# Attention scores of two heads as one pair: 64-row tiles, two banks, maximum and shift for two units

## The reference, cut

```python
# sliding window attention (SWA), 8 query heads on 2 key heads of 64, window 128
s = einsum('bnqhgd,bnkhd->bnhgqk', qb, kk) * ATTN_SCALE
s = where(valid, s, NEG)
m = maximum(max(s, -1), sink)
p = exp(s - m);  p = p / (sum(p) + exp(sink - m))
# forgetting attention (fox), 8 heads of 64, causal
s = einsum('bqhd,bkhd->bhqk', q_blk, k) * ATTN_SCALE
s = s + c_blk[..., None] - c[:, :, None, :]
s = where(k_pos <= q_pos, s, NEG)
p = softmax(s);  o = einsum('bhqk,bkhd->bqhd', p, v)
```

## Time and profile before

| | us |
|---|---|
| median of 3 runs (1494.97 to 1495.83) | 1495.04 |
| span of the profiled execution | 1495.9 |
| TensorE busy | 1349.3 |
| VectorE busy | 479.2 |
| ScalarE busy | 264.3 |
| attention loop, first score load to first output transpose | 87.7 |

### The profile page before, as it was taken

How to read it: one execution, slowest core, us unless ns; L and a number is a source line. 1 busy time by engine, 2 the same in 40 slices (tenths; PEclk the granted TensorE clock), 3 DMA queues, 4 the chain that set the end, 5 groups by cost and what they waited for, 6 DMA issues and landing times.

```text
span 1495.9 us, 27925 instructions
## 1 busy us (share of the span) xinstructions
PE 1349.3 (90%) x11152; PEld 653.5 (44%) x11152; DVE 479.2 (32%) x1212; ACT 264.3 (18%) x452; POOL 168.6 (11%) x250
## 2 busy tenths in 40 slices
PE   6999998999969999989898898989889898989986
PEld 5998887878943333223232222323222232322221
DVE  4122747766354232222322222232222223222211
ACT  4223436433221011001011000101100011110001
POOL 2001401000010111111110111111011111101111
PEclk9999999999979999999999999999999999999998
DMA  6222320002658999999999999999999999999997
GB/s 183 85 84 85 107 90 1 1 29 85 254 208 309 390 407 401 402 402 406 404 401 411 395 408 402 407 403 403 409 397 407 402 406 404 404 408 397 407 401 244
DMA packets 112807, 458.14 MB, mean 306 GB/s; under 512 B 12129, under 2 KB 37761, under 8 KB 79969
## 3 DMA queue, kind: packets, MB, share of 16 engines
q1 hardware_dynamic: 102736, 433.87, 73.1%
q0 software_dynamic: 9344, 21.37, 5.9%
q10 hardware_dynamic: 688, 2.38, 0.4%
HBM read 442.90 MB, written 14.68 MB: 306 GB/s over the span
## 4 chain that ended last, share of the span: by engine, by line
PE 42%; DMA 27%; SPq 26%; DVE 2%; issue 2%; ACT 1%; POOL 0%; DVEq 0%; POOLq 0%; ACTq 0%
DMA gu_tail<-in_w_gate_up_dram 26%; SPq L474 15%; SPq L470 10%; PE ps L1607 8%; PE ps L1646 3%; PE ps L1342 3%; PE ps L1343 3%; PE ps L1344 3%; PE ps L1351 3%; PE ps L1352 3%; PE ps L1353 3%; PE ps L1438 2%; PE ps L1465 2%; PE ps L1652 1%; PE ps L1634 1%
## 5 line engine op out<-in xcount | busy, mean ns | idle before, releaser
L1607 PE MATMUL ps<-gu_head,xT 128*32 128x512 f32 x3840 | 440.0, 600 | 74.5 <-DMA gu_head<-in_w_gate_up_dram 70.0
L1607 PEld LDWEIGHTS ps<-gu_head,xT 128*32 128x32 f32 x3840 | 115.7, 110 | 392.2 <-issue 235.6
L1646 PE MATMUL ps<-wdn,aT 128*32 128x512 f32 x2048 | 237.9, 594 | 12.7 <-DMA wdn<-in_w_down_dram 10.8
L1166 DVE TENSOR_REDUCE row_f<-ps 128x2 f32<-128x4 f32 (+1 forms) x33 | 5.3, 161 | 525.8 <-PE ps L1572 525.8
L1607 PE MATMUL ps<-gu_tail,xT 128*32 128x512 f32 x1280 | 146.8, 595 | 16.4 <-DMA gu_tail<-in_w_gate_up_dram 16.3
L807 ACT COPY gu_tok<-ps 128x512 f32<-128x512 f32 x80 | 46.8, 585 | 621.3 <-PE ps L1607 621.3
L1646 PEld LDWEIGHTS ps<-wdn,aT 128*32 128x32 f32 x2048 | 62.0, 110 | 156.8 <-issue 126.3
L611 POOL DMA_INDIRECT xg_a<-h_dram,idx_g x33 | 33.3, 1008 | 580.2 <-DVE idx_all L1169 296.5
L860 DVE TENSOR_TENSOR st_l<-st_w,st_h 128x2048 fp32r<-128x2048 f32 x25 | 57.3, 2292 | 120.5 <-ACT st_h L683 120.5
L1607 PEld LDWEIGHTS ps<-gu_tail,xT 128*32 128x32 f32 x1280 | 37.1, 109 | 125.1 <-issue 63.5
L1342 PE MATMUL ps<-st_h,hT_h 128*128 128x256 f32 x288 | 82.4, 286 | 2.0 <-DVE hT_l L875 2.0
(11 more groups left out here) (337 smaller groups left out, 1588.9 us busy)
## 6 DMA issues: line engine op xcount, KB each, us to landing
gu_head<-in_w_gate_up_dram SPq DMA_DIRECT2D x192, 1024.0 KB, 21.1
wdn<-in_w_down_dram SPq DMA_DIRECT2D x128, 1024.0 KB, 26.7
gu_tail<-in_w_gate_up_dram SPq DMA_DIRECT2D x64, 1024.0 KB, 26.8
st_w<-in_w_in_dram SPq DMA_DIRECT2D x17, 1024.0 KB, 5.3
st_w<-in_w_out_dram SPq DMA_DIRECT2D x4, 1024.0 KB, 5.1
x_tok<-in_x_dram SPq DMA_DIRECT2D x4, 512.0 KB, 6.1
st_w<-in_w_o_swa_dram SPq DMA_DIRECT2D x4, 512.0 KB, 3.6
st_w<-in_w_o_fox_dram SPq DMA_DIRECT2D x4, 512.0 KB, 4.6
```

The source lines that it names most:

```text
L1607: ins = pe.matmul(ps[j * GROUP:(j + 1) * GROUP, n, :], xT[:, k, n * GROUP:(n + 1) * GROUP], gu_chunk(k)[:, j * 512:(j + 1) * 512], start=( ...
L1646: ins = pe.matmul(ps[u * GROUP:(u + 1) * GROUP, 4, :], aT[:, 2 * j + k, u // 2 * GROUP:(u // 2 + 1) * GROUP], wdn[:, j, k, u % 2 * 512:(u ...
```

## The change

The two heads of a pair (2p, 2p+1) are computed together. The wide query tiles go; `qaT` and `qfT` hold two heads one above the other, as the keys do, and each head's matmuls read and load only its 64 rows. The two heads write two banks, and their instructions alternate; from 384 columns on the scores come in pieces of 256 columns, below in pieces of 128. The bias comes first for fox, the mask first for SWA. `c_pick` gets its ones on the lower 64 rows also, by two more selects. One semaphore increment stands for both scores; VectorE takes the maximum over two banks and one shift for two units (`sink_neg` replaces `sink8`). `p_sb` has four buffers and lies elsewhere. The orders of TensorE and VectorE in the loop are new. A turned query block goes out as one block of 128 rows, and the zero fills are gone.

```diff
         def turned(s, j):
             bank = ps[:, QKT_BANK[QKT.index((s, j)) % 4], :]
-            if s % 2:
-                return [((None, kaT, None, kfT)[s][:, j, :], bank, 1.0 if s < 2 else g_fx[:, 1:2])]
-            out = []
-            for a in (0, 1):
-                rows = slice(a * HD, (a + 1) * HD)
-                out.append((wide_q(s == 2, 2 * j + a)[rows, :], bank[rows, :], 1.0 if s < 2 else g_fx[rows, 0:1]))
-            return out
+            return (qaT, kaT, qfT, kfT)[s][:, j, :], bank, (1.0, 1.0, g_fx[:, 0:1], g_fx[:, 1:2])[s]
...
-            for row in range(0, HD, 32):
+            for row in range(0, P, 32):
                 then(g.affine_select(out=c_pick[:, :], in_=c_pick[:, :], compare_op=ALU.not_equal, fill=1.0,
...
-            pool.wait_ge(group_done, G_O)
-            for half in (0, 1):
-                other = slice((1 - half) * HD, (2 - half) * HD)
-                for part in (qa_lo, qa_hi):
-                    g.memset(part[other, half::2, :], 0.0).then_inc(q_zeroed, 1)
...
             for n in range(NU):
-                act.wait_ge(shift, n + 1)
-                if n >= 3:
-                    act.wait_ge(pT_ps, n - 2)
+                act.wait_ge(shift, n // 2 + 1)
+                if n >= 4:
+                    act.wait_ge(pT_ps, n - 3)
...
-            for n in range(NU + 5):
-                if n < NU:
...
+            for p in range(NP + 3):
+                if p < NP:
+                    n = 2 * p
                     c, b, h = units[n]
-                    dve.wait_ge(scores, n + 1)
-                    v.reduce_max(mx[:, n:n + 1], ps[:, n % 4, 0:width(n)], AX.X).then_inc(maxed, 1)
...
+                    two, bank, w = slice(n, n + 2), n % 4, width(n)
+                    dve.wait_ge(scores, p + 1)
+                    v.tensor_reduce(mx[:, two], ps[:, bank:bank + 2, 0:w], AX.X, ALU.max).then_inc(maxed, 1)
+                    dve.wait_ge(maxed, p + 1)
                     if b == 0:
...
+                        v.scalar_tensor_tensor(out=nb[:, two], in0=mx[:, two], scalar=-SCALE, in1=sink_neg[:, h:h + 2],
+                                               op0=ALU.mult, op1=ALU.min).then_inc(shift, 1)
                     else:
...
+                        v.tensor_scalar(nb[:, two], mx[:, two], -SCALE, None, ALU.mult).then_inc(shift, 1)
...
+                if 1 <= p <= NP:
+                    for m in (2 * p - 2, 2 * p - 1):
+                        dve.wait_ge(pT_ps, m + 1)
+                        if m >= 2:
+                            dve.wait_ge(pv_done, m - 1)
+                        v.tensor_copy(pT_sb[:, m % 2, 0:width(m)], ps[:, 4 + m % 2, 0:width(m)]).then_inc(pT_ready, 1)
...
-            def unit_scores(n):
+            def pair_scores(p):
+                n = 2 * p
                 c, fox, h = units[n]
+                w = width(n)
                 k0 = (c + 1) * P - w
+                piece = 256 if w > 256 else P
+                if p >= 2:
+                    pe.wait_ge(probs, n - 2)
+                for a in (0, 1):
+                    rows, bank = slice(a * HD, (a + 1) * HD), (n + a) % 4
+                    if fox:
+                        pe.matmul(ps[:, bank, 0:w], c_pick_r[rows, h + a:h + a + 1].broadcast_to([HD, P]),
+                                  c_rows[rows, 0:w], start=True, stop=False)
+                    else:
+                        m = mask_b[:, :, :].rearrange("p a k -> p (a k)")[:, 2 * P - w:2 * P]
+                        pe.matmul(ps[:, bank, 0:w], ident_b[:, :], m, start=True, stop=False)
+                for at in range(0, w, piece):
+                    end = min(at + piece, w)
+                    for a in (0, 1):
+                        rows = slice(a * HD, (a + 1) * HD)
+                        q = (qfT if fox else qaT)[rows, h // 2, c * P:(c + 1) * P]
+                        kv = kfT[rows, h // 2, k0 + at:k0 + end] if fox else kaT[rows, h // (HQ // KV), k0 + at:k0 + end]
+                        ins = pe.matmul(ps[:, (n + a) % 4, at:end], q, kv, start=False, stop=(not fox and end == w))
                 if fox:
+                    for a in (0, 1):
+                        ins = pe.matmul(ps[:, (n + a) % 4, w - P:w], ident_b[:, :], mask_b[:, 1, :], start=False, stop=True)
                 ins.then_inc(scores, 1)
...
-            for n in range(NU + 3):
...
+            for p in range(NP + 2):
+                if p < NP:
+                    pair_scores(p)
+                if 1 <= p <= NP:
+                    unit_transposes(2 * p - 2)
+                if p >= 2:
+                    unit_values(2 * p - 3)
+                if 1 <= p <= NP:
+                    unit_transposes(2 * p - 1)
+                    unit_values(2 * p - 2)
```

More of the change, by code:

```diff
@@ L127, in hybrid_block @@
         stage.rewind(16 * K)
-        qa_lo = stage.put("qa_lo", [P, HQ // 2, T])
-        stage.rewind(32 * K)
-        qa_hi = stage.put("qa_hi", [P, HQ // 2, T])
+        qaT = stage.put("qaT", [P, HQ // 2, T])
         stage.rewind()
@@ L155, in hybrid_block @@
         kaT = r1.put("kaT", [P, KV, T])
-        qf_wide = r1.put("qf_wide", [P, HF, T])
+        qfT = r1.put("qfT", [P, HF // 2, T])
         kfT = r1.put("kfT", [P, HF // 2, T])
+        p_sb = r1.put("p_sb", [P, 4, T])
         r1.rewind()
@@ L190, in hybrid_block @@
         work.rewind()
-        p_sb = work.put("p_sb", [P, 3, T])
         pT_sb = work.put("pT_sb", [P, 2, T])
@@ L248, in hybrid_block @@
         sink_bc = const.put("sink_bc", [P, HQ])
-        sink8 = const.put("sink8", [P, HQ])
+        sink_neg = const.put("sink_neg", [P, HQ])
         brt = const.put("brt", [P, E])
@@ L404, in hybrid_block @@
         NU = len(units)
+        NP = NU // 2
         QKT = [(s, j) for s in range(4) for j in range((HQ // 2, KV, HF // 2, HF // 2)[s])]
         QKT_BANK = (4, 5, 2, 3)
-        def wide_q(fox, h):
-            return qf_wide[:, h] if fox else (qa_lo, qa_hi)[h // 4][:, h % 4]
         def turned(s, j):
             bank = ps[:, QKT_BANK[QKT.index((s, j)) % 4], :]
-            if s % 2:
-                return [((None, kaT, None, kfT)[s][:, j, :], bank, 1.0 if s < 2 else g_fx[:, 1:2])]
-            out = []
-            for a in (0, 1):
-                rows = slice(a * HD, (a + 1) * HD)
-                out.append((wide_q(s == 2, 2 * j + a)[rows, :], bank[rows, :], 1.0 if s < 2 else g_fx[rows, 0:1]))
-            return out
+            return (qaT, kaT, qfT, kfT)[s][:, j, :], bank, (1.0, 1.0, g_fx[:, 0:1], g_fx[:, 1:2])[s]
         def width(n):
@@ L592, in _ @@
                 g.tensor_tensor(hs_r[:, c, :], hs_sum[:, c, :], minus_half[:, c, :], ALU.pow).then_inc(hs_rstd, 1)
-            pool.wait_ge(group_done, G_O)
-            for half in (0, 1):
-                other = slice((1 - half) * HD, (2 - half) * HD)
-                for part in (qa_lo, qa_hi):
-                    g.memset(part[other, half::2, :], 0.0).then_inc(q_zeroed, 1)
-            for half in (0, 1):
-                other = slice((1 - half) * HD, (2 - half) * HD)
-                g.memset(qf_wide[other, half::2, :], 0.0).then_inc(q_zeroed, 1)
             pool.wait_ge(group_done, G_END)
@@ L744, in _ @@
                 act.wait_ge(qkT_ps, n + 1)
-                for dst, src, scale in turned(s, j):
-                    ins = sc.activation(dst, src, ACT.Identity, scale=scale)
-                ins.then_inc(qkT_out[1], 1)
+                dst, src, scale = turned(s, j)
+                sc.activation(dst, src, ACT.Identity, scale=scale).then_inc(qkT_out[1], 1)
             for n in range(NU):
-                act.wait_ge(shift, n + 1)
-                if n >= 3:
-                    act.wait_ge(pT_ps, n - 2)
+                act.wait_ge(shift, n // 2 + 1)
+                if n >= 4:
+                    act.wait_ge(pT_ps, n - 3)
                 w = width(n)
-                sc.activation(p_sb[:, n % 3, 0:w], ps[:, n % 4, 0:w], ACT.Exp, bias=nb[:, n:n + 1],
+                sc.activation(p_sb[:, n % 4, 0:w], ps[:, n % 4, 0:w], ACT.Exp, bias=nb[:, n:n + 1],
                               scale=SCALE, accum_out=den[:, n:n + 1]).then_inc(probs, 1)
@@ L990, in _ @@
                 dve.wait_ge(qkT_ps, n + 1)
-                for dst, src, scale in turned(s, j):
-                    ins = v.tensor_scalar(dst, src, scale, None, ALU.mult)
-                ins.then_inc(qkT_out[0], 1)
+                dst, src, scale = turned(s, j)
+                v.tensor_scalar(dst, src, scale, None, ALU.mult).then_inc(qkT_out[0], 1)
             def finish_block(u):
@@ L1022, in _ @@
                     if b == 0:
-                        v.tensor_scalar(nb[:, n:n + 1], mx[:, n:n + 1], sink8[:, h:h + 1], -SCALE,
-                                        ALU.max, ALU.mult).then_inc(shift, 1)
-                    else:
[L1026 to L1029, removed]
@@ L1030, in _ @@
-                if n >= 12 and (n - 12) % 8 == 0:
-                    finish_block((n - 12) // 8)
```

(26 more changed lines are left out.)

17 lines of the change are left out of this document (1 added, 16 removed).

## The result

The changed kernel takes 1512.65 us (median of 4, 1509.59 to 1514.85) where the kernel before takes 1495.01: a ratio of 1.0114, 95% interval 1.0102 to 1.0126. It is slower by 17.6 us; the forecast was slower by 7. The direction and the ring were right, the size was not.

What follows compares the result with a forecast made beforehand. TensorE's order bounds the loop before, a closed ring of scores, maximum, shift, copy and values after. Loop +9.4 us and evacuation -2.6 make +6.8 on 1495.04, say 1502.0 us; own range 1498.5 to 1506.

Steps and rivals of the forecast that it cites:

- the ring: Attention loop: scores, maximum over two banks, shift, copy, values wait on each other without overlap; loop 97.0 us instead of 87.65.
- The ring's periods: Time per pair in the loop, scores + 0.48 + maximum + copy + values: 1.92 (SWA 128) to 4.71 us (fox 512).
- the change of tiles: Scores: switching TensorE between whole array and 64-row tiles costs 0.20 us in, 0.15 back to the 16-bit mask.
- the maximum over two banks: VectorE in the loop: a pair's maximum reads twice the columns, 0.42 us for 256 up to 1.23 for 1024.
- Rivals 2, 3 and 4: Changing tiles costs nothing (1493.2, 0.10); two heads' loads do not overlap (1513, 0.13); tiles run nothing side by side (1519, 0.08).
- the sum: Whole forecast: loop +9.4 us, evacuation -2.6, together +6.8, giving 1502.0 us; its loop is 97.0 us.
- the first pair has only its scores: Loop's start: 1.4 us taken off the total of the pairs' periods for the first pair.
- The evacuation: Turned queries written as whole blocks before the loop: 2.6 us gained, with 0.2 us allowed for TensorE's transposes.
- Rival 5: TensorE's clock falls in the loop's gaps; 24 us at the low level adds some 12 us: 1514, chance 0.03.
- the range: Forecast's own total, 1498.5 to 1506 us, explained as 0.2 us on each of 31 rings; chance 0.56.
- Rival 1: TensorE stays the loop's bound, faster: loop 79 us, total 1483.5 us, chance 0.10.
- the estimate of 2 to 3 us more: Score steps at 384 and 512 columns a quarter to a third longer, by the skill page; sum near 1504.

Runs made afterwards that it cites:

- e1: Changed kernel with TensorE computing the values of unit 2p-2 one pair later, behind the next pair's scores: 1483.68 us.
- e3: Changed kernel with five idle matmuls filling TensorE's gap before the values of 2p-2, in the first eight pairs only: 1506.73 us.
- e2: Changed kernel with five idle matmuls filling TensorE's gap before the values of 2p-2, in every pair: 1505.04 us.
- e4: Changed kernel without the 64-row tiles: wide queries with zeros, one whole-array matmul per head, same order: 1519.18 us.
- e10: Changed kernel with idle matmuls in the gaps of pairs 4 to 8 only, the first three pairs unfilled: 1506.64 us, one run.

## Why the prediction was right or wrong, point by point

- **What bounds the loop.** Right: TensorE before, the ring after, TensorE again once the order is mended (e1).
- **The ring's periods.** Right within 0.03 us wherever a steady pair runs at full clock: in e3's profile 1.90 for SWA 128 (sum 1.92), 2.10 for fox 128 (2.12), 2.85 for SWA 256 (2.86), 2.96 for fox 256 (2.96), 3.85 (3.83), 4.74 (4.71), read as the distance between maxima. With that each link is confirmed: the side by side loads and streams of two row tiles (eight loads in 0.52 us, not 0.9), the change of tiles, the maximum over two banks at twice the columns (1.225 us for 1024 by the groups, 1.23 expected). Rivals 2, 3 and 4 are gone.
- **The loop at full clock.** 99.1 us in e3, where the sum had 97.0. Start to start, the first two pairs take 3.06 us instead of 2.45, and 0.24 of that is e3's filling (the second maximum to the third takes 2.50 there, 2.26 in the changed kernel). The sum left out 0.5: with "the first pair has only its scores" it also dropped that pair's copy and values, which the ring runs one pair later. The four pairs with VectorE's sink sum (L1001) take 0.20 us more each, 0.8 together, because it stands between shift and copy. The tail is 0.3 longer. `finish_block` costs nothing: behind its division VectorE still waits for the next scores, and the pair takes 3.85 us like the one before it. In e3:

```profile
235.49 0.16 DVE L995 SCALAR_TENSOR_TENSOR nb<-mx,sink_neg 128x2 f32<-128x2 f32 x1
235.69 0.17 DVE L1001 TENSOR_TENSOR snk<-sink_bc,nb 128x8 f32<-128x8 f32 x1
235.77 0.48 DVE L1007 COPY pT_sb<-ps 128x128 f32<-128x128 f32 x2
...
290.69 0.69 DVE L982 TENSOR_TENSOR o_tok<-ps,rden 128x512 f32<-128x512 f32 x1
292.10 0.96 DVE L992 TENSOR_REDUCE mx<-ps 128x2 f32<-128x768 f32 x1 [0.72 <-PE ps L1434]
```

- **The evacuation.** 1.9 us of the 2.6. The changed kernel's rows show the rest:

```profile
226.28 1.06 ACT L725 ACTIVATE qaT<-ps 128x512 f32<-128x512 f32 x2
...
227.30 3.52 PEld L1405 LDWEIGHTS ps<-ident,tok 128*128 128x128 f32 x32
...
229.35 0.69 ACT L725 ACTIVATE qfT<-ps,g_fx 128x512 f32<-128x512 f32 x1 [0.19 <-PE ps L1405]
230.23 0.69 ACT L725 ACTIVATE kfT<-ps,g_fx 128x512 f32<-128x512 f32 x1 [0.19 <-PE ps L1405]
231.10 0.69 ACT L725 ACTIVATE kfT<-ps,g_fx 128x512 f32<-128x512 f32 x1 [0.19 <-PE ps L1405]
```

  The blocks take 0.69 us, as priced, but start 0.87 apart, each with 0.19 to 0.28 us of waiting for TensorE. It makes 32 transposes without a pause in 3.52 us, 0.44 a block, and each of the two writing engines takes every second block: at the end TensorE sets the pace. I had allowed 0.2 us for its transposes altogether.
- **The clock.** This is the step that failed. Rival 5 was there, with a chance of 0.03. I argued from the earlier trace rows: two microseconds with a third of the work kept the full clock, two without any lost it. Those rows say nothing of a loop that runs thinly for many microseconds. So the sum put the effect of the ring's gaps on the clock at nothing. In fact the clock fell in both profiles of the changed kernel and cost it 7 to 8 us (107.0 and 106.4 against 99.1 in e3), the largest part of the miss: of the spans' +16.2 against +6.8, the clock is 7.9, the loop at full clock 2.1, the evacuation 0.7, and the stages outside -1.3. Without the clock the sum would be 1502.0 + 2.8 = 1504.8, inside the range; e2, with all gaps filled, has 1505.04. I had priced a low stretch at 12 us for 24, and no row gave its length. The 27 to 31 us cost less because only TensorE's links of the ring slow. That rival 5's total of 1514 came close is in part luck: its price was some 4 us too high, and 2.8 us were missing elsewhere.
- **The range.** "0.2 us on each of 31 rings" is 6 us either way; the stated range allowed about 4.
- **What I took for the busy share.** In the first 3.6 us of the loop the changed kernel shows TensorE busy for 2.94, 82%, and then loses the clock; e4 shows 3.00 in the same stretch of its loop and 77% over its first eight pairs, and keeps it. The busy row counts a matmul's whole modelled length, and two that run side by side are as long as one. It was no measure of the work.
- **Rival 1** did not happen in the changed kernel, but e1 is what it describes: with the order mended the loop is 77.8 us and the total 1483.68, where that rival had 79 and 1483.5.
- **The Trainium skill's rules.** The drain on a change of tiling mode ("TensorEngine Tiling (Array Packing)", Key Properties) is seen: about 0.1 us before the first 64-row load, in the pair shown. The 3.07 for four tiles ("TensorE: Matmul & The Clock Gate", Part 3, Measured speedup) did not carry over: the pairs of 384 and 512 columns took 3.85 and 4.74 us where full overlap of two row tiles gave 3.83 and 4.71, and the estimate of 2 to 3 us more was not needed. That page's Part 4 on transposes and the clock is neither borne out nor refuted here, since every loop mixes them with matmuls.

What stays open: which quantity the clock goes by. The profiles show that the clock falls with tiles and gaps (twice), that it falls without tiles when the gaps are longer, and that it holds with tiles when the gaps are filled or gone. That array time decides is argued: it fits all of them, and rows in use or instructions in a time were not told apart. Where in the loop the clock falls is seen in one profiled execution for each kernel, two for the changed one; of the others only the mean is known.

## What to carry to other kernels

When two units are fused into one step, write down each engine's list and look for the ring: a wait on a copy that stands behind a maximum of the step just issued took more than side by side matmuls gave, and moving one call past the next scores turned 1.1% slower into 0.8% faster. When work is made faster and the engine then waits, ask what happens to TensorE's clock over the whole stretch, and judge by the work in it, not by the busy row. Set the small per-block instructions against the ring too: one between its links costs its time (the sink sum, 0.20 us), one that falls where the engine waits costs nothing (the division).

## What the hardware showed that I had not expected

- The clock fell to 1.2 GHz behind 3.6 us in which TensorE's row is 82% busy, and idle matmuls that lengthen TensorE's list made the whole kernel shorter by 6 to 8 us (1512.65 to 1506.73 and 1505.04).
- The fall lasts: 27 to 34 us at the lower level, also through pairs whose gaps were harmless at full clock; with filled pairs from the fourth on it was back after 6.9 us (e10, one execution).
- Two 64-row tiles load and stream side by side without loss: eight loads in 0.52 us, and at 1024 columns for two heads the pair's period met the sum within 0.03 us.
